# A hybrid attention block on one core: the rotary embedding moved to GpSimd and small DMAs, and the plain fp32 products joined into fewer bursts

## The reference

```
h = rms_norm(x) * norm_g
qa ka va za qb kb vb zb ga gb = split(h @ w_in)      # widths 512 128 128 512 512 512 512 512 1024 1024
qa, ka = partial_rope(...)                            # the first 16 of each head's 64 channels
ya = sliding_window_attention(qa, ka, va, sinks) * silu(za)   # 8 query heads, 2 key heads, chunks of 64, 1 back
yb = chunked_attention(qb, kb, vb, rel_bias) * silu(zb)       # 8 heads, own chunk and 8 before, with a bias
out = rms_norm(x + (sigmoid(ga + b0) * (ya @ w_br_a) + sigmoid(gb + b1) * (yb @ w_br_b)) @ w_out) * final_g
```

## Time and profile before

| | us |
|---|---|
| median of 3 runs (3415.64 to 3418.3) | 3417.24 |
| the profiled execution | 3415.78 |
| its span, first to last instruction | 3414.0 |
| PE busy | 3342.3 |
| DVE busy | 1488.9 |
| ACT busy | 1422.8 |
| POOL busy | 1306.6 |

### The profile page before, as it was taken

How to read it: one execution, slowest core, us unless ns; L and a number is a source line. 1 busy time by engine, 2 the same in 40 slices (tenths; PEclk the granted TensorE clock), 3 DMA queues, 4 the chain that set the end, 5 groups by cost and what they waited for, 6 DMA issues and landing times.

```text
span 3414.0 us, 48305 instructions
## 1 busy us (share of the span) xinstructions
PE 3342.3 (98%) x16328; PEld 2498.0 (73%) x16328; DVE 1488.9 (44%) x3097; ACT 1422.8 (42%) x2969; POOL 1306.6 (38%) x1087
## 2 busy tenths in 40 slices
PE   8999999999999999999999999999999999999998
PEld 6667876678766787667876678766787667876676
DVE  4662355513555135551355513555135551355512
ACT  4443444434444344443444434444344443444432
POOL 3334442345423454234542344423454234542244
PEclk9999999999999999999999999999999999999999
DMA  4222431224311242112421124311242112521123
GB/s 156 62 62 87 172 99 50 62 87 167 99 50 62 87 168 99 50 62 87 168 99 52 61 86 168 98 56 61 83 172 94 55 60 84 173 93 56 56 82 116
DMA packets 97782, 319.53 MB, mean 94 GB/s; under 512 B 9984, under 2 KB 26624, under 8 KB 95360
## 3 DMA queue, kind: packets, MB, share of 16 engines
q1 hardware_dynamic: 97536, 316.34, 28.4%
HBM read 299.52 MB, written 16.78 MB: 93 GB/s over the span
## 4 chain that ended last, share of the span: by engine, by line
PE 85%; issue 6%; DVE 5%; POOL 2%; ACT 1%; DMA 0%; DVEq 0%; POOLq 0%; SPq 0%; ACTq 0%
PE acc L909 16%; PE acc L911 14%; PE acc L910 14%; PE ps_o L1004 6%; PE ps_pt L973 5%; PE sc L953 4%; PE sc L909 3%; PE sc L910 3%; PE sc L911 3%; POOL w_lo L755 2%; PE sc L944 2%; PE sc L851 2%; PE sc L852 2%; PE sc L853 2%; PE sc L876 1%
## 5 line engine op out<-in xcount | busy, mean ns | idle before, releaser
L755 POOL TENSOR_TENSOR w_lo<-w_raw,w_hi 128x512 fp32r<-128x512 f32 x928 | 1209.2, 1309 | 2060.0 <-ACT w_hi L1058 2059.3
L909 PE MATMUL acc<-h_hi,w_hi 128*128 128x512 f32 x2432 | 1010.4, 415 | 2.4 <-DVE q L1316 2.4
L911 PE MATMUL acc<-h_hi,w_lo 128*128 128x512 f32 x2432 | 952.7, 392 | 0.0
L910 PE MATMUL acc<-h_lo,w_hi 128*128 128x512 f32 x2432 | 950.4, 391 | 0.0
L1058 ACT ACTIVATE w_hi<-w_raw 128x512 fp32r<-128x512 f32 x928 | 574.2, 624 | 392.9 <-DMA w_raw<-w 116.5
L909 PEld LDWEIGHTS acc<-h_hi,w_hi 128*128 128x128 f32 x2432 | 456.3, 188 | 212.3 <-issue 133.9
L911 PEld LDWEIGHTS acc<-h_hi,w_lo 128*128 128x128 f32 x2432 | 456.4, 188 | 101.5
L910 PEld LDWEIGHTS acc<-h_lo,w_hi 128*128 128x128 f32 x2432 | 458.1, 188 | 75.7
L1146 ACT ACTIVATE probs_b<-sc,negm 128x640 f32<-128x640 f32 x256 | 203.2, 794 | 373.6 <-DVE negm L1263 373.0
L1153 ACT ACTIVATE probs_t<-ps_pt 128x512 f32<-128x512 f32 (+1 forms) x272 | 150.7, 554 | 264.8 <-PE ps_pt L973 264.8
L1288 DVE SCALAR_TENSOR_TENSOR part<-th,sc 128x512 f32<-128x512 f32 x64 | 43.9, 686 | 468.0 <-PE sc L911 467.8
(11 more groups left out here) (140 smaller groups left out, 3923.8 us busy)
## 6 DMA issues: line engine op xcount, KB each, us to landing
w_raw<-w SPq DMA_DIRECT2D x464, 512.0 KB, 3.5
rows<-x SPq DMA_DIRECT2D x36, 512.0 KB, 7.4
xt<-x_t SPq DMA_DIRECT2D x16, 1024.0 KB, 10.0
out<-rows SPq DMA_DIRECT2D x32, 512.0 KB, 2.8
x_in<-x SPq DMA_DIRECT2D x28, 512.0 KB, 5.4
cs<-rope_tab SPq DMA_DIRECT2D x8, 512.0 KB, 4.3
bias<-near SPq DMA_DIRECT2D x1, 1024.0 KB, 13.3
g_out<-final_g SPq DMA_DIRECT2D x1, 512.0 KB, 11.5
```

The lines of the kernel that those rows point to most:

```text
L755: pool.tensor_tensor(w_lo[n % 2][:, c], w_raw[n % 2][:, c], w_hi[n % 2][:, c].bitcast(FP32), ALU.subtract).then_inc(w_split, 1)
L909: pe.matmul(dst[:, :], hi, src_hi[:, k, :], start=begin, stop=False)
L910: pe.matmul(dst[:, :], hi, src_lo[:, k, :], start=False, stop=False)
L911: mm = pe.matmul(dst[:, :], lo, src_hi[:, k, :], start=False, stop=end)
```

## The change

The partner's channels are brought over by DMA instead of by PE. After ACT's copy to `pre`, SP issues four DMAs of eight partitions each, which put channels i + 8 of `pre` to i of `rot` and i to i + 8, for both heads; the rest of `rot` is zero from the start (or is zeroed once per block, for the second buffer, which lies over another tile). POOL multiplies `pre` by the cosines into its destination, then `rot` by the sines (the sign is now in the table) and adds. `pre_hi`, `pre_lo`, the permutation, and the rotation's use of the `acc` banks are gone. `pre` and `rot` have two buffers each.

In the order of work: the scores of pair 0 start two quarters later, the filler's `rope` step one quarter later, and in the beats values 0 and 1, and 2 and 3 (A), and 0 and 1, and 5 and 6 (B) now stand together, so that a pair of each kind has nine runs of plain fp32 products instead of thirteen.

```diff
-A_BEATS = "T0 F G T1 V0 F H D T2 V1 S0 F E0 T3 V2 F S1 V3 F E1 F F S2 F E2 F F S3 F E3 F"
-B_BEATS = "F T0 F G T1 F H D T2 V0 F T3 F T4 V1 S0 F T5 E0 F T6 V2 S1 F T7 E1 F T8 V3 S2 F T9 E2 V4 S3 T10 F E3 V5 F V6"
+A_BEATS = "T0 F G T1 F H D T2 V0 V1 S0 F E0 T3 F F S1 V2 V3 F E1 F S2 F E2 F F S3 F E3 F"
+B_BEATS = "F T0 F G T1 F H D T2 F T3 F V0 V1 S0 T4 F T5 E0 F T6 V2 S1 F T7 E1 F T8 V3 S2 F T9 E2 V4 S3 T10 F E3 F V5 V6"
...
-        at_ = QUARTERS * O_TILES + 14 + t
+        at_ = QUARTERS * O_TILES + 16 + t
...
-            fill[at_ + 2] = [("rope", s), *fill[at_ + 2]]
+            fill[at_ + 3] = [("rope", s), *fill[at_ + 3]]
...
-USES_ACC = ("job", "turn_v", "rope_k", "rope", "norm")
+USES_ACC = ("job", "turn_v", "norm")
...
+    pre = [at(f"pre{i}", [P, BLK], FP32, y_lo_at + 4 * BLK * n) for i, n in enumerate((3, 6))]
+    rot = [sb("rot0", [P, BLK]), at("rot1", [P, BLK], FP32, y_lo_at + 4 * BLK * 7)]
...
+            def swap(b, step):                     # SP, at the end of k0, q0, q1, q2, q3
+                i = ROPE_NO[("rope_k" if step[1] == "k" else "rope", step[2])] % 2
+                wait_freed(sp, b, step)
+                for h0 in (0, HD):
+                    for to, src in ((h0, h0 + HALF_ROT), (h0 + HALF_ROT, h0)):
+                        sp.dma_start(rot[i][to:to + HALF_ROT, :], pre[i][src:src + HALF_ROT, :]).then_inc(rope_swapped[i], 16)
...
+                    if step == ("mm", TILES.index(("k", 0)), 0):      # POOL
+                        hold(h_done, (b + 1) * KT)
+                        pool.memset(rot[1][:, :], 0.0).then_inc(rot_zeroed, 1)
...
+                    elif step[0] in ("rope_in", "rope_in_k"):
...
+                        pool.tensor_tensor(roped(step), pre[no % 2][:, :], cs[:, 0, :], ALU.mult).then_inc(rope_cos, 1)
+                    elif step[0] in ("rope", "rope_k"):
...
+                        pool.wait_ge(rope_swapped[no % 2], b * (64 * (3 - no % 2)) + 64 * (no // 2 + 1))
+                        pool.tensor_tensor(rot[no % 2][:, :], rot[no % 2][:, :], cs[:, 1, :], ALU.mult).then_inc(rope_sin, 1)
+                        pool.wait_ge(rope_sin, b * NROPE + (no + 1))
+                        pool.tensor_tensor(roped(step), roped(step), rot[no % 2][:, :], ALU.add).then_inc(rope_done, 1)
...
-                        pe.matmul(bank(step)[:, :], perm_r[:, :], pre_hi[:, :], start=True, stop=False)
-                        pe.matmul(bank(step)[:, :], perm_r[:, :], pre_lo[:, :], start=False,
-                                  stop=True).then_inc(acc_full, 1)
...
-                    act.activation(pre_hi[:, :], pre[:, :], ACT.Copy).then_inc(rope_hi, 1)
...
-                        dve.tensor_tensor(pre_lo[:, :], pre[:, :], pre_hi[:, :].bitcast(FP32),
-                                          ALU.subtract).then_inc(rope_lo, 1)
-                        dve.tensor_tensor(pre[:, :], pre[:, :], cs[:, 0, :], ALU.mult).then_inc(rope_cos, 1)
...
-                        dve.tensor_tensor(dst, bank(step)[:, :], cs[:, 1, :], ALU.mult).then_inc(free(step), 1)
-                        dve.tensor_tensor(dst, pre[:, :], dst, ALU.add).then_inc(rope_done, 1)
```

More of the change, by code:

```diff
@@ L31 @@
 HD = 64
+HALF_ROT = HD // 8
 PAIRS = 4
@@ L360, with program @@
 check_ring()
-def program(nc, x, x_t, w, near, far, sinks, norm_g, final_g, gate_b, rope_tab, perm, eye, out):
+def program(nc, x, x_t, w, near, far, sinks, norm_g, final_g, gate_b, rope_tab, eye, out):
     off = [(nc.sbuf_base + 63) // 64 * 64]
@@ L408, in program @@
     y_lo_at = y_at + 4 * SETS * BLK
-    pre = at("pre", [P, BLK], FP32, y_lo_at + 4 * BLK * 3)
-    pre_lo = at("pre_lo", [P, BLK], FP32R, y_lo_at + 4 * BLK * 6)
-    pre_hi = at("pre_hi", [P, BLK], FP32R, y_lo_at + 4 * BLK * 7)
+    pre = [at(f"pre{i}", [P, BLK], FP32, y_lo_at + 4 * BLK * n) for i, n in enumerate((3, 6))]
     bias = sb("bias", [P, 9, A_KEYS])
@@ L427, in program @@
     ident = sb("ident", [P, P])
-    perm_raw = sb("perm_raw", [P, P])
-    perm_r = sb("perm_r", [P, P], FP32R)
+    rot = [sb("rot0", [P, BLK]), at("rot1", [P, BLK], FP32, y_lo_at + 4 * BLK * 7)]
     far_sb = sb("far_sb", [P, 8])
@@ L487, in program @@
     pair_valued = sem("pair_valued")
-    rope_hi = sem("rope_hi")
-    rope_lo = sem("rope_lo")
+    rope_swapped = [sem(f"rope_swapped{i}") for i in range(2)]
     rope_cos = sem("rope_cos")
+    rope_sin = sem("rope_sin")
+    rot_zeroed = sem("rot_zeroed")
     rope_done = sem("rope_done")
@@ L519, in program @@
     c_dve = sem("c_dve")
-    N_CONSTS = 6
+    N_CONSTS = 5
     ADDED = HALVES * TT - O_BANKED
@@ L685, in _ @@
             load_w(0, 1)
-            for dst, src in ((perm_raw[:, :], perm), (g_out[:, :], final_g), (bias[:, 0:8, :], near), (far_sb[:, :], far),
+            for dst, src in ((g_out[:, :], final_g), (bias[:, 0:8, :], near), (far_sb[:, :], far),
                              (sink_sb[:, :], sinks), (gb_raw[:, :], gate_b)):
@@ L689, in _ @@
             sp.dma_start(cs[:, :, :], rope_tab[0]).then_inc(cs_in, 16)
+            sp.wait_ge(zeroed, 6)
             def body(b, first, last):
@@ L694, in body @@
                         load_w(b, step[1] + 2)
+                    elif step[0] == "job" and step[1] in ("k", "q") and step[2] < PAIRS:
+                        swap(b, step)
                     elif step == ("scores", ORDER[-1], 0) and not last:
@@ L731, in _ @@
             pool.memset(v_b[:, 0:TT, :], 0.0).then_inc(zeroed, 1)
-            pool.wait_ge(zeroed, 5)
+            pool.memset(rot[0][:, :], 0.0).then_inc(zeroed, 1)
+            pool.wait_ge(zeroed, 6)
             def rsqrt(which, t, n, got, got_count, mid, done, count):
@@ L756, in split_lo, with roped @@
                                    ALU.subtract).then_inc(w_split, 1)
+            def roped(step):
+                return k_a[:, P:P + BLK] if step[0].endswith("_k") else q[POS[step[1]] % 2][:, :]
             rsqrt_x(0)
@@ L782, in body @@
                             pool.tensor_copy(v_b[:, 0:TT, c:c + P], v_b[:, TT:2 * TT, c:c + P]).then_inc(kept, 1)
+                    elif step[0] in ("rope_in", "rope_in_k"):
+                        job_ = ("job", "k" if step[0] == "rope_in_k" else "q", step[1])
+                        bank_, k = WHERE[job_]
+                        hold(acc_free[bank_], b * ON_BANK[bank_] + (k + 1))
+                        if step[0] == "rope_in_k" and not first:
+                            hold(kept, (b - 1) * NKEEP + (KEEP_NO[("keep_k", PAIRS - 1)] + 1))
+                        pool.wait_ge(cs_in, 16 * (b + 1))
+                        no = ROPE_NO[(step[0].replace("_in", ""), step[1])]
+                        pool.tensor_tensor(roped(step), pre[no % 2][:, :], cs[:, 0, :], ALU.mult).then_inc(rope_cos, 1)
+                    elif step[0] in ("rope", "rope_k"):
+                        no = ROPE_NO[step]
+                        hold(rope_cos, b * NROPE + (no + 1))
+                        pool.wait_ge(rope_swapped[no % 2], b * (64 * (3 - no % 2)) + 64 * (no // 2 + 1))
+                        pool.tensor_tensor(rot[no % 2][:, :], rot[no % 2][:, :], cs[:, 1, :], ALU.mult).then_inc(rope_sin, 1)
+                        pool.wait_ge(rope_sin, b * NROPE + (no + 1))
+                        pool.tensor_tensor(roped(step), roped(step), rot[no % 2][:, :], ALU.add).then_inc(rope_done, 1)
                     elif step[0] == "next_rstd" and not last:
@@ L826, in _ @@
             turn_rstd(0)
-            pe.wait_ge(zeroed, 5)
+            pe.wait_ge(zeroed, 6)
             def token_products(b, n, c):
@@ L1020, in body @@
                         products(b, first, step[1], step[2])
-                    elif kind in ("rope", "rope_k"):
-                        claim(b, step)
-                        pe.wait_ge(rope_lo, b * NROPE + (ROPE_NO[step] + 1))
-                        pe.matmul(bank(step)[:, :], perm_r[:, :], pre_hi[:, :], start=True, stop=False)
-                        pe.matmul(bank(step)[:, :], perm_r[:, :], pre_lo[:, :], start=False,
-                                  stop=True).then_inc(acc_full, 1)
                     elif kind == "scores":
@@ L1095, in job_done @@
                     no = ROPE_NO[("rope_k" if name == "k" else "rope", idx)]
-                    if not (first and no == 0):
-                        act.wait_ge(rope_done, b * NROPE + no)
-                    act.activation(pre[:, :], ps, ACT.Copy,
+                    if not first or no >= 2:
+                        act.wait_ge(rope_done, b * NROPE + max(no - 1, 0))
+                    if no == 1:
+                        act.wait_ge(rot_zeroed, b + 1)
+                    act.activation(pre[no % 2][:, :], ps, ACT.Copy,
                                    scale=SCALE if name == "q" else 1.0).then_inc(free(step), 1)
-                    wait_freed(act, b, step)
-                    act.activation(pre_hi[:, :], pre[:, :], ACT.Copy).then_inc(rope_hi, 1)
                 elif name == "k":
@@ L1221, in _ @@
             dve.wait_ge(consts_in, 16 * N_CONSTS)
```

(30 more changed lines are left out.)

## The result

| | before | after |
|---|---|---|
| median, us | 3416.44 (4 runs, 3415.22 to 3418.3) | 3384.21 (4 runs, 3383.46 to 3385.77) |
| profiled execution, us | 3415.78 | 3383.46 |
| PE busy, us | 3342.3 | 3293.6 |
| POOL busy, us | 1306.6 | 1458.6 |
| mean granted clock of PE | 0.999 | 0.992 |

The ratio is 0.9906, with a 95% interval from 0.9892 to 0.992. The kernel became faster by 32 us; forecast were 66 us, and the time lies 10 us outside the range. So about half of the gain is missing, and the first question is where.

What follows compares the result with a forecast made beforehand. TensorE, busy 98% of the span, was taken as the bound, through its own steps. Terms 18.8 + 11.3 + 4.1 + 22.0 + 5.2 + 1.8 = 63.2 us off 3415.8 gave 3352.6, stated as 3350; range 3338 to 3374.

Steps and rivals of the forecast that it cites:

- Products of the rotation and the waits that go with them: On TensorE: 40 rotations' products go (18.8 us), with waits at gate, bank, values 0 and last exponential (11.3, 4.1, 5.2, 1.8).
- the 5.2 us: Values 0 of an A pair, now two quarters later, no longer waits for VectorE to read the pair before: 5.2 us.
- The 1.8 us: Scores 3 no longer waits 0.26 us behind ScalarE's deleted second rotation copy, once in each of 7 blocks: 1.8 us.
- Bursts: Joining plain fp32 steps on TensorE saves 116 changes into and out of plain fp32, at 0.19 us each: 22.0 us.
- Rival B: On TensorE, the plain fp32 price is paid per step, so joining gives nothing: 3374.6 us; chance 0.06.
- The added work hides: POOL's rotation work and SP's swap DMAs delay nothing, even at a block's start, with 2.9 and 2.7 us cover: nothing lost.
- the chain: Block start, from the end of k0's products: copy +0.9, issues +2.2, landing +5.7, POOL done +14.8, before scores 0 at +17.7 us.
- rival A: POOL comes late at a block's head, its operations reaching 2.34 us: 3356 to 3386 us, between them 3371; chance 0.11.
- the 3.5 that I took: Landing time of a 16 KB swap copy inside SBUF, taken from a 512 KB weight load in running traffic: 3.5 us.
- rival C: Swap DMAs land late and delay scores at a block's head; slower from 14.3 us landing, 3429 at 16 us; chance 0.04.
- Scores 2 behind scores 1: In B pairs, scores 2 needs banks back after 5.2 us, and 5.85 us lie between: cover 0.65 us, costed at nothing.

Runs made afterwards that it cites:

- The rotation alone, without the stall: Changed kernel with the old orders of the beats and with weight loads issued ahead of the swap DMAs on SP; 3376.47 us, ratio 0.9882.
- the run with the copy first: Changed kernel, but ScalarE copies finished tiles k0, q0 and v0 before splitting the weights of two tiles ahead; 3333.26 us, ratio 0.9752.
- the kernel with the loads first: Changed kernel, but SP issues a rotation's four swap DMAs one step later, behind the next weight load; 3333.56 us, ratio 0.9754.
- two DMAs: Changed kernel, but each rotation issues two of its four swap DMAs, leaving out half of the exchanged channels; 3349.78 us, ratio 0.9806.

## Why the prediction was wrong, step by step

- **Products of the rotation and the waits that go with them** (18.8 + 11.3 + 4.1 + 5.2 + 1.8 = 41.2 us): right in sum. The rotation alone, without the stall, gained 40.5. The reason given for the 5.2 us, the later place of values 0, is enough but not needed: the wait goes with the new beats alone and with the rotation's move alone. The 1.8 us did not show in the total: the seven waits of 0.26 us are gone, but the row is 3.7 us against 3.6, because waits in the first block grew (to 0.98 and 1.20 at most) and the last block has two new ones.
- **Bursts** (22.0 us): the mechanism was right, the size was not. Measured are 42.9 us. This error runs against the next one and hides part of it: with the bursts as forecast, the kernel would have been slower by another 21 us. The prediction priced going in and out (0.18 to 0.20), which the earlier trace rows show; it did not ask whether a step of values is shorter behind another one. Rival B fell, on the other side than feared.
- **The added work hides** (0 us): this is the step that failed. "The next weight load stands behind them, at most one tile later than now, and is still one tile ahead of its use" holds for TensorE, as the run with the copy first shows, and fails for ScalarE, which reaches the split of that load before it copies the finished tile. The copies, whose end the chain puts 0.9 us behind their products (it is 0.8 in the kernel with the loads first), then come late, and so does the next swap. I followed what stands behind the swap on SP, but not what stands behind the load on the next engine. The issue time was taken from large loads, 0.34 us; a swap's was 0.67. Price: 50.6 us, of which some 16 are the clock, which no rival had.
- **GpSimd** (rival A): its part was forecast well. By source line, duration in ns, min/median/max:
```profile
L816 POOL TENSOR_TENSOR rot<-rot,cs x40: 1262/1285/1604, 52.5 to 3122.7; 128x512 f32<-128x512 f32 x40
L818 POOL TENSOR_TENSOR q<-q,rot x32: 1261/1284/1353, 61.4 to 3124.3; 128x512 f32<-128x512 f32 x32
```
 Priced were 1.29 us, and 1465 us busy against 1458.6; the longest is 1.60, not 2.34. The first swap's last issue ended at 1713.26 (1710.58 + 2.68) and GpSimd went on at 1714.67: landing at most 1.4 us after the issues, not the 3.5 that I took, so rival C was far off. Counted from the start of the last issue (0.62 us long) it is 2.0 us. The Trainium skill (DMA: Bandwidth & Descriptors, section on the anatomy of one DMA) gives about 2 us fixed, for DMAs that GpSimd issues; the trace agrees for this one from SP, with 2.0 us.
- **Scores 2 behind scores 1** (cover 0.65 us): held nearly everywhere: in blocks 2 to 7 PE no longer waits for the exponentials at all. The last block has two such waits (0.18 and 0.34 us), and those of the first block are the longer ones named above.
- The parts are 40.5 + 42.9 - 50.6 = 32.8 us, against 32.2 from before to after. They are differences along one path of runs and so have to add up; that they do is no proof of them.

Two things stay open: why an issue of 8 partitions holds SP twice as long as a weight load, and why a run of values or scores pays its 0.15 or 0.20 us once.

## What to carry to other kernels

A step put into an in-order queue must be followed through every queue that it delays, not only to its last user: the late load was early enough for TensorE, but stood ahead of an urgent copy on ScalarE. Issue what must wait for new data behind what could go at once, and finished results ahead of work for later; either order alone gave back 51 us here. When steps are merged, compare the pitch of a step behind its own kind with that of a step alone, and look at each queue that serves them (VectorE's copies) again.

## What the runs showed of the hardware that was not expected

- Four DMAs of 16 KB, 8 partitions of 2 KB each, held SP for 2.68 us; a 512 KB load of 128 partitions held it for 0.34 us.
- Of eight stops of PE of 2.2 to 2.5 us, seven left the granted clock at 1.00 and one, of 2.47 us, was followed by 0.50. Eight of 3.07 to 4.67 us (the kernel with the new beats only) and eight of 4.9 to 5.2 us (the changed kernel) were all followed by 0.50.
- What the longer stop at the turn cost beyond its longer idle time was the products at the lower clock: 1.3 to 2.8 us a block in the changed kernel, and nothing in the seven blocks with two DMAs where the clock stayed at 1.00.
- In plain fp32, two joined values steps (of 4 products each, 256 columns) took 1.02 us against 2 x 0.58, and two joined scores steps (of 4, 192 columns) 0.86 against 2 x 0.53.
